# A fp32 decoder trunk: column-wise FFN products with stationary weight pieces, and a dilated attention layer in four residue classes

## The reference, cut to what matters

```
for i in range(4):                                  # kinds: stick-breaking, sliding window, dilated, stick-breaking
    x = LN(a*x + 0.5*swiglu(x, ffn1_w_in[i], ffn1_w_out[i]))
    x = LN(a*x + mixer_i(x))
    x = LN(a*x + 0.5*swiglu(x, ffn2_w_in[i], ffn2_w_out[i]))
    x = x + sigmoid(x @ ple_w_gate[i]) * (p[i] @ ple_w_proj[i])

def swiglu(x, w_in, w_out):                         # w_in 1024 x 5632, w_out 2816 x 1024
    gate, up = split(x @ w_in, 2)
    return (silu(gate) * up) @ w_out

def dilated(x, w_in, w_out):                        # three groups of 16 heads of 64, layer 2 only
    for (win, dil) in ((128, 1), (512, 4), (2048, 16)):
        q, k, v = rope(q), rope(k), v               # of the group
        # token t sees t - dil*n for n = 0 .. win//dil, softmax per group, and its log-sum
    return merge(the three outputs by the softmax of their log-sums) @ w_out
```

## Time and profile before

| | us |
|---|---|
| median of 3 runs | 2258.08 (2257.26 to 2260.7) |
| the profiled execution: its own time | 2257.6 |
| its span | 2255.5 |
| PE busy in the span | 2223.3 |
| PEld busy | 1823.4 |
| DVE busy | 1324.5 |
| ACT busy | 1084.1 |
| DMA, share of 16 engines' span | 54.3% |

### The profile page before, as it was taken

One profiled execution on the slowest core, in us unless ns is written; L12 is line 12 of the kernel. 1 busy time (PEld: TensorE's weight loads), 2 busy tenths in 40 slices (PEclk: granted clock), 3 DMA queues, 4 the chain that ended last, 5 costly groups with the idle time before them and its releaser, 6 DMA issues.

```text
span 2255.5 us, 26355 instructions
## 1 busy us (share of the span) xinstructions
PE 2223.3 (99%) x10756; PEld 1823.4 (81%) x10756; DVE 1324.5 (59%) x1598; ACT 1084.1 (48%) x1340; POOL 18.0 (1%) x53
## 2 busy tenths in 40 slices
PE   8999999999999899999999999999999999999999
PEld 7888878888888678888888878878888888888887
DVE  5446575456545864556446766765456545666546
ACT  5444564445444654445444453454445444565433
POOL 0000000000000000000000000000000000000000
PEclk9999999999999999999999999999999999999999
DMA  8654546555654365647564544546555654546552
GB/s 294 193 179 151 175 133 207 189 186 185 207 186 150 131 203 180 198 134 236 187 200 144 174 142 140 178 127 210 186 191 178 209 191 150 168 150 205 178 188 105
DMA packets 212936, 401.44 MB, mean 178 GB/s; under 512 B 12368, under 2 KB 30928, under 8 KB 212688
## 3 DMA queue, kind: packets, MB, share of 16 engines
q1 hardware_dynamic: 212816, 399.76, 54.3%
HBM read 398.66 MB, written 1.05 MB: 177 GB/s over the span
## 4 chain that ended last, share of the span: by engine, by line
PE 89%; DVE 6%; ACT 2%; DMA 2%; issue 1%; POOL 0%; SPq 0%; ACTq 0%; DVEq 0%; POOLq 0%
PE ps L1110 26%; PE ps L1112 26%; PE ps L1111 26%; PE ps L1153 4%; DVE wl L775 2%; PE ps L1218 1%; PE ps L1217 1%; PE ps L1216 1%; ACT wh L501 1%; DMA raw<-in_ple_w_gate 1%; PE ps L1338 1%; PE ps L1441 1%; PE ps L1357 1%; DMA raw<-in_sb_w_in 0%; ACT arena L553 0%
## 5 line engine op out<-in xcount | busy, mean ns | idle before, releaser
L775 DVE TENSOR_TENSOR wl<-raw,wh 128x1024 fp32r<-128x1024 f32 x730 | 867.2, 1222 | 482.4 <-ACT wh L501 478.1
L501 ACT ACTIVATE wh<-raw 128x1024 fp32r<-128x1024 f32 x730 | 752.3, 1058 | 592.3 <-PE ps L1112 413.5
L1110 PE MATMUL ps<-wh,xh 128*128 128x512 f32 x2064 | 813.7, 394 | 4.7 <-DVE xl L782 4.7
L1112 PE MATMUL ps<-wh,xl 128*128 128x512 f32 x2064 | 804.4, 390 | 0.0
L1111 PE MATMUL ps<-wl,xh 128*128 128x512 f32 x2064 | 803.8, 389 | 0.0
L1110 PEld LDWEIGHTS ps<-wh,xh 128*128 128x128 f32 x2064 | 388.7, 188 | 86.0 <-DVE xl L782 6.4
L1112 PEld LDWEIGHTS ps<-wh,xl 128*128 128x128 f32 x2064 | 388.3, 188 | 81.0
L1111 PEld LDWEIGHTS ps<-wl,xh 128*128 128x128 f32 x2064 | 388.9, 188 | 76.7
L1110 PE MATMUL ps<-wh,hth 128*128 128x512 f32 x736 | 289.5, 393 | 0.0
L1112 PE MATMUL ps<-wh,htl 128*128 128x512 f32 x736 | 287.1, 390 | 0.0
L1111 PE MATMUL ps<-wl,hth 128*128 128x512 f32 x736 | 286.7, 390 | 0.0
(11 more groups left out here) (108 smaller groups left out, 1111.0 us busy)
## 6 DMA issues: line engine op xcount, KB each, us to landing
raw<-in_ffn_w_in SPq DMA_DIRECT2D x352, 512.0 KB, 4.6
raw<-in_ffn_w_out SPq DMA_DIRECT2D x176, 512.0 KB, 4.5
raw<-in_dil_w_in SPq DMA_DIRECT2D x72, 512.0 KB, 4.3
raw<-in_sb_w_in SPq DMA_DIRECT2D x48, 512.0 KB, 4.7
raw<-in_ple_w_gate SPq DMA_DIRECT2D x32, 512.0 KB, 4.8
raw<-in_sb_w_out SPq DMA_DIRECT2D x16, 512.0 KB, 5.2
gb<-in_ln_g SPq DMA_DIRECT2D x12, 512.0 KB, 6.6
gb<-in_ln_b SPq DMA_DIRECT2D x12, 512.0 KB, 7.3
```

The lines of the kernel that those rows point to most:

```text
L501: act.activation(wh[:, u % RING, :], raw[:, u % RAWS, :], ACT.Copy).then_inc(hi_done, 1)
L775: dve.tensor_tensor(wl[:, u % RING, :], raw[:, u % RAWS, :], wh[:, u % RING, :].bitcast(F32), ALU.subtract).then_inc(lo_done, 1)
L1110: pe.matmul(out_, a_h, b_h, start=start, stop=False)
L1112: return pe.matmul(out_, a_l, b_h, start=False, stop=stop)
```

## The change

**FFN.** The first 512 hidden columns are made as before. The other 2304 are now nine pieces of 256 columns. In `by_column` the weights are the stationary operand (128 rows by 128 columns of `wh` or `wl`) and the transposed activations the moving one: `wh` meets high and low activations side by side in one matmul of 512 columns (two halves of 256 tokens), `wl` meets the high ones in one of 256. The result has the hidden index on partitions; its two 256-column halves in a bank must be added. DVE does this with a `tensor_reduce` over both, once for gate (`gate_sum`) and once for up (in `hidden`), then multiplies (all in SBUF); ACT writes `hth` straight from the result, DVE `htl`. Their transposes are gone; those of block 0 (8 in an FFN) stay. Units: 4 for a piece (2 gate, 2 up) and 2 for its down product, which follows one piece later, at the end two. A unit is now read from HBM as 4 row chunks of 256 columns in place of 2 of 512.

**Dilated layer.** Tokens are stored in four residue classes of 64. A query tile has two classes; within groups 1 and 2 a query only meets the keys of its own class, so that the scores of a step have 256 + 64 + 64 = 384 columns. `z` makes them with 2 matmuls of 256 columns and 8 of 64x64 in place of 4 of 128x128; `tr` has 6 transposes, not 8; `av` has 4 matmuls of 128 columns and 4 of 64, where one stacked operand holds a group-1 class in half of its partitions and a group-2 class in the other half. The values of groups 1 and 2 are copied by two DVE instructions each. v of these groups is projected from `hth`/`htl`, into which ACT and DVE copy `xh` and `xl` once, in the order of the classes.

```diff
-NJ = FF // BLK
+SUB = 256
+NJ = (FF - BLK) // SUB
-DW = 4 * P
+DW = 3 * P
+CLS = 4
+CW = S // CLS
+def ffn_base(j):
+    return 8 * j if j < 2 else 6 * j + 4 - 2 * (j == NJ)
+def h_slot(j):
+    return 2 * ((j + 1) % 3) if j else 0
...
# SP, loads of an FFN
+                for j in range(1, NJ + 1):
+                    for col in (0, FF):
+                        for k in (0, 4):
+                            load(win, k, BLK + (j - 1) * SUB + col, SUB)
+                    if j == 1:
+                        down(0), down(2)
+                    elif j < NJ - 1:
+                        down(2 * j)
...
# ACT
+            def hidden_hi(i, j):
+                act.wait_ge(h_done.sem, h_done.at(i, j))
+                act.activation(hth[:, h_slot(j):h_slot(j) + 2].rearrange("p c t m -> p c (t m)"), hs, ACT.Copy).then_inc(th_done.sem, 1)
+                for j in range(1, NJ + 1):
+                    b = ffn_base(j)
+                    to(u0, b + 8)
+                    silu(i, j)
+                    to(u0, b + 10 + (j < NJ))
+                    hidden_hi(i, j)
+                            if late == ("q", 0, 2):
+                                wait(act, tl_done, "x", i, 1, 1)
+                                act.activation(classes(hth), by_class(xh), ACT.Copy).then_inc(xph_done.sem, 1)
...
# DVE
+            def gate_sum(i, j):
+                dve.wait_ge(w_used, ends["gate", i, j])
+                dve.tensor_reduce(gs, ps[:, 0:2, :].rearrange("p c (r n) -> p c n r", r=2), AX.X, ALU.add).then_inc(gs_done.sem, 1)
+            def hidden(i, j):
+                dve.wait_ge(w_used, ends["up", i, j])
+                if j:
+                    own(dve.tensor_reduce(us, ps[:, 2:4, :].rearrange("p c (r n) -> p c n r", r=2), AX.X, ALU.add))
+                    dve.wait_ge(silu_done.sem, silu_done.at(i, j))
+                    ins = dve.scalar_tensor_tensor(hs, gs, 0.5, us, ALU.mult, ALU.mult)
...
+                    to(u0, b + 8)
+                    gate_sum(i, j)
                     to(u0, b + 10)
+                    hidden(i, j)
+                    to(u0, b + 10 + (j < NJ))
+                    hidden_lo(i, j)
...
+                    for r in range(2):
+                        at = r if g == 1 else 1 - r
+                        ins = dve.tensor_copy(vst[at * CW:(at + 1) * CW, r:CLS:2, :], ps[r * CW:(r + 1) * CW, pair:pair + 2, :])
...
+                                dve.tensor_copy(classes(htl), by_class(xl)).then_inc(xpl_done.sem, 1)
...
# PE
+            def by_column(half, bank):
+                ready(u)
+                for c in range(2):
+                    for k in range(4):
+                        n = 4 * half + k
+                        w_h, w_l = (view(w, u % RING, SUB)[:, k, c * P:(c + 1) * P] for w in (wh, wl))
+                        x_h, x_hl = (xhl[:, n, 0:r].rearrange("p r t m -> p (r t m)") for r in (1, 2))
...
+                            pe.matmul(ps[:, bank + c, 0:SUB], w_l, x_h, start=False, stop=False)
+                            ins = pe.matmul(ps[:, bank + c, :], w_h, x_hl, start=False, stop=n == 7)
+                ins.then_inc(w_used, 1)
...
+                        pe.wait_ge(gs_done.sem, gs_done.at(i, j - 1))
+                    by_column(0, 0)
+                    if j == 1:
+                        hidden_t(i)
+                    by_column(1, 0)
+                    pe.wait_ge(h_done.sem, h_done.at(i, j - 1))
+                    by_column(0, 2)
+                    by_column(1, 2)
+                    if j < NJ - 1:
+                        down(j - 1)
...
# PE, dilated layer, z
-                    for g, keys, at in ((0, slice(0, S), 0), (1, own, S), (2, own, S + P)):
+                    for m in range(2):
+                        pb = slice(HD * m, HD * (m + 1))
+                        pe.matmul(ps[:, bank + m, 0:S], qT[pb, 0, c, t * P:(t + 1) * P], kT[pb, 0, c, :], start=True, stop=True)
+                    for g in (1, 2):
+                        for r in range(2):
+                            own = slice((2 * t + r) * CW, (2 * t + r + 1) * CW)
+                            at = S + CW * ((g - 1) ^ r)
+                            for m in range(2):
+                                pb = slice(HD * m, HD * (m + 1))
+                                ins = pe.matmul(ps[r * CW:(r + 1) * CW, bank + m, at:at + CW], qT[pb, g, c, own], kT[pb, g, c, own],
+                                                start=True, stop=True)
```

More of the change, by code:

```diff
@@ L1223, in ffn @@
                 run(col_items(2, BLK), False)
-                for j in range(1, NJ):
-                    g = col_items(0, BLK)
-                    pe.wait_ge(silu_done.sem, silu_done.at(i, j - 1))
-                    run(g[0:3], False)
-                    hidden_t(i, j - 1, 4)
-                    run(g[3:4], False)
-                    pe.wait_ge(tl_done.sem, tl_done.at("h", i, j - 1))
-                    run(y_items(4, hth, htl, first=j == 1, last=False), False)
-                    run(col_items(2, BLK), False)
@@ L1244, in ffn @@
+                down(NJ - 2)
+                pe.wait_ge(tl_done.sem, tl_done.at("h", i, NJ - 1))
+                y0 = y_items(2, hth, htl, chunk0=h_slot(NJ - 1), first=False, last=False)
+                y1 = y_items(2, hth, htl, chunk0=h_slot(NJ), first=False)
+                run([y0[0], y1[0], y0[1], y1[1]], True, y=(1, 3),
                     before=closing(i, lambda t, n: wait(pe, tl_done, "h", i, NJ) if (t, n) == (0, 1) else None))
@@ L1352, in av @@
                     c, t = s // NT, s % NT
-                    for n, (g, kb) in enumerate(((0, 0), (0, 1), (1, t), (2, t))):
+                    for kb in range(2):
                         for m in range(2):
@@ L1379, in dil @@
                             pending = what, hh, g
-                    v0, v1, v2 = (col_items(bank_of("dil", "v", hh, g), BLK, *((xph, xpl) if g else (xh, xl))) for g in range(NG))
+                    v0, v1, v2 = (col_items(bank_of("dil", "v", hh, g), BLK, *((hth, htl) if g else (xh, xl))) for g in range(NG))
                     if hh == 1:
@@ L1550, in constants @@
     put("swa", np.concatenate(banded(lambda d: (d >= 0) & (d <= 127)), 1))
-    order = (NT * np.arange(P)[None, :] + np.arange(NT)[:, None]).reshape(-1)
+    own = CLS * np.arange(CW)
     masks = []
-    for tile in order.reshape(NT, P):
-        for (window, step), keys in zip(DIL, (np.arange(S), tile, tile)):
-            d = tile[:, None] - keys[None, :]
-            masks.append(np.where((d >= 0) & (d % step == 0) & (d // step <= window // step), 0.0, NEG))
+    for tile in range(NT):
+        rows = []
+        for r in range(2):
+            mine = own + 2 * tile + r
+            groups = ((0, np.arange(S)), (1 + r, mine), (2 - r, mine))
+            cols = []
+            for g, keys in groups:
+                window, step = DIL[g]
+                d = mine[:, None] - keys[None, :]
+                cols.append(np.where((d >= 0) & (d % step == 0) & (d // step <= window // step), 0.0, NEG))
+            rows.append(np.concatenate(cols, 1))
+        masks.append(np.concatenate(rows, 0))
     put("dil", np.concatenate(masks, 1))
```

237 lines of the change are left out of this document (117 added, 120 removed).

## The result

The changed kernel takes 2246.7 us (median of five, 2246.15 to 2248.0) where the kernel before took 2257.9 beside it: a ratio of 0.9949, 95% interval 0.9938 to 0.9961. It is faster by 11.2 us, about half of the 21.2 forecast, inside the range, and 1.9 us from what the first rival gives. The profiled execution took 2246.15, its span is 2244.2.

A forecast was written before the change was run, and what follows sets the result against it. The prediction took PE's stream of matmuls as the bound. FFN products +16.2, transposes -32.4, late low half -2.6 and dilated layer -2.4 summed to -21.2 us, from 2257.6 to 2236.4 us; the 8-in-10 range was 2225 to 2253 us.

The forecast's parts named there:

- the first rival: FFN products: alternation keeps wide products slow, 0.3524 us a pair, sum -9.0, time 2248.6 us; chance 0.20.
- FFN, products: Matmuls of the 2304 changed columns: wide and narrow pairs at 0.3471 us in place of 512-column products, +16.2 us.
- FFN, transposes: 36 of 44 transposes on PE's queue vanish from each of 8 FFNs, 0.1125 us each: -32.4 us.
- The late low half: FFN down product no longer waits for `htl` behind transposes, 32 times 0.08 us: -2.6 us.
- FFN, DVE, ACT and DMA at nothing: FFN reductions, splits, new waits and 1 KB row loads stay hidden behind PE's work: costed at nothing.
- Dilated layer, steps: The 16 steps of `z`, `tr` and `av` each get 0.16 us shorter: -2.6 us, from -7.0 to +5.1.
- A pair of passes at 64 columns: Dilated steps: two heads' narrow passes side by side, between 0.055 and 0.11 us, taken as 0.07.
- The 0.1 for one more change of array shape: Dilated layer, `z`: one extra change of array shape costs +0.1 us a step, 0 to 0.1.
- Dilated layer, beside the steps: Dilated layer outside the steps: v projection -1.2, value copies +2.4, ends of halves -1.0 us.
- The copies at the first `av`: Dilated layer: two value copies of 1.22 us for one delay the first `av` of both halves, +2.4 us.
- The stride: Dilated v of groups 1 and 2: contiguous weights save 0.006 us on each of 192 products, -1.2 us.
- The ends of the halves: Dilated layer: PE's 3.3 us of waits for the division shrink by about a third, -1.0 us (0 to -3.3).

The follow-up runs named there:

- run8: Changed kernel with the products of the 256-column pieces ordered eight wide, then eight narrow, instead of alternating: 2233.8 us, ratio 0.9896 to the kernel before.
- tr2x: Kernel before with each of its 44 transposes of an FFN made twice, 352 more on PE: 2293.15 us, ratio 1.0158.
- sum2x: Changed kernel with both DVE reductions of a piece made twice: 2254.98 us, ratio 0.9987 to the kernel before.
- mid_split: Kernel before with DVE's last split of an FFN moved between the first tile's two residual additions: 2255.2 us, ratio 0.9988.
- run8_vact: Kernel run8 with one of the two value copies of group 2 moved from DVE to ACT: 2231.9 us, ratio 0.9886 to the kernel before.
- run2: Changed kernel with wide and narrow products of the 256-column pieces ordered two by two: 2236.8 us, ratio 0.9911 to the kernel before.
- vstride: Changed kernel with v of dilated groups 1 and 2 projected from activations read at a step of two again: one traced execution, 2250.56 us.

## Why the prediction was half right

- **FFN, products: the step that failed.** "I take 0.3471" per pair; measured 0.3525, and the term is +28.6 for +16.2. This is the first rival's case, the price of alternation. That its 0.3524 is met so closely is in part luck: it put the wide one at 0.232 and the narrow one at 0.1204, and they take 0.2357 and 0.1176. Right in the step were the fixed part of 0.0133, the narrow product at 0.12 and the hidden load. Wrong was the ground on which I set the rival at 0.20: that the slow state "ends after five wide products, as if a backlog were worked off". The row was read rightly, for `run8` shows the same debt, 27 ns behind a run. But in an alternating stream nearly every wide product has a narrow one ahead of it, so no run is long enough to leave that state: 5.8 ns are paid in each of 2304 pairs, 13.4 us, and 3.1 more in the down products behind. Of these 16.5 `run8` keeps 144 debts of 27 ns, 3.9 us, and gave 12.9 back by order alone.
- **FFN, transposes.** -32.4 forecast, -31.7 by the timelines, whose 0.109 for a transpose gives `tr2x`'s time as well, once the vanished wait is counted.
- **The late low half.** The wait of the earlier trace rows on `htl` behind the transposes is gone. The -2.6 was not tested by itself.
- **FFN, DVE, ACT and DMA at nothing.** No wait on a reduction inside an FFN, the reduction at 1.224, the queue's share at 55.5%. The step held for pieces and missed the ends. Even two passes for a reduction, 22.3 us of DVE to 22.2 of PE in the last two pieces, were costed at nothing there; `sum2x` is that case, and it cost 8.3 us. And two terms stood in no row of the sum: PE's wait on `x`, -4.3 (worth 2.95 in `mid_split`), and the wake of the narrow products in the down products, +3.1. With them and the forecast's terms for the rest, 28.6 - 32.4 - 2.6 - 4.3 + 3.1 = -7.6, or -6.3 with the 2.95, against -6.95 measured.
- **Dilated layer, steps.** 2.65 for 2.95 us: -7.6 for -2.6, and beyond my lower end of -7.0. "A pair of passes at 64 columns" was bounded below by half of 0.11 for two heads; the 16 passes in 0.40 us show four at a time. The Trainium skill (TensorEngine Tiling, Tiling Modes) lists 64x64 as four tiles; the trace agrees, with that 0.40. Had I read the shape in the change, 64 rows by 64 columns, as a quarter, the bound would have held. The 0.1 for one more change of array shape was right: from the last wide pass of the scores to the first narrow one it is 0.306 us, 0.209 before.
- **Dilated layer, beside the steps.** The copies at the first `av`: +2.4 as forecast, and `run8_vact` gave 2.5 back. The stride: -0.8 for -1.2. The ends of the halves: 3.5 us of waits for 3.3, so the -1.0 did not come; with faster steps PE arrives earlier and waits the longer for the division. The two copies of `xh` and `xl` by class cost nothing, as forecast: PE did not wait for them. A wait of 1.2 us that stood in no term came at the layer's end, where ACT and DVE write the output of the second half in a wider step (L624 and L1033 above). The sum, -7.6 + 2.4 - 0.8 + 0.2 + 1.2 = -4.6, against -4.4 measured.

So the 11.2 us are a miss of 12.4 in one term, softened by 2 in the dilated layer and 1.2 at the FFN's boundaries; 0.7 more has no term. The total fell inside the range because that range took in the first rival, and because the misses beside it went the other way.

Left open: why a wide product behind a narrow one takes 9 ns more and the narrow one only gives 2.4 back. No run here separates the array, the load and the write to PSUM. The price is not a fixed one for each change from narrow to wide: over 0.3467 a pair it is 6.6 ns for each of the 2016 changes of the kernel after, 5.2 for each of the 1008 of `run2`, and 27 for each of the 144 of `run8`, whose wide runs are long enough to pay it in full. Nor does it belong to narrow products alone: behind transposes, too, products take 0.230, 0.236, 0.229 and 0.232 us after the first, ahead of 0.2267.

## What to carry to other kernels

A rate read in a uniform stream is the price of a uniform stream: where a change interleaves two shapes, take the rate of the first products behind the seam as the likeliest, not as a rival, and write the order so that equal shapes stand together. When the rows and the columns of a product both fall to half the array, price it by how many fit side by side. An engine with slack in the middle of a stage can still be the last at its end, so look at the boundary before an addition to it is booked at nothing. And where tokens are stored in a new order, price the instructions that write them back as well as those that use it.

## What the runs showed of the hardware that was not expected

- Alternating products of 512 and 256 columns cost 0.3525 us a pair, in runs of eight 0.3467 and 27 ns for each change from narrow to wide, two by two 0.349, at a granted clock of 1.0.
- Sixteen fp32 passes on 64x64 tiles of 64 columns take 0.40 us, 0.025 each.
- A DVE split of 1.22 us on 128x1024 holds up a POOL instruction on 128x1 that starts beside it: 1.05 to 1.14 us for 0.19.
- A reduction of pairs over 1024 PSUM elements a partition takes 1.224 us, as long as the copy.
- A stationary operand read at a step of two elements lengthens a product of 512 columns, 0.2327 us for 0.2267, though its load is hidden (before, `vstride`).
- Writes of 128x1024 from PSUM to SBUF at a step of four elements took 2.02 us on ACT and 2.05 on DVE, at a step of two 1.10 and 1.23 (one row each).
